# Weight slabs from one array in order of use, the low half written over the landed slab, four landing slots

## The reference

```
# first block, layers 0 and 1
mix = diff_moba_mixer(x, ...) if l == 0 else gla_mixer(x, ...)
x = layer_norm(DEEPNORM_ALPHA * x + mix, ln_mix_g[l], ln_mix_b[l])
x = layer_norm(DEEPNORM_ALPHA * x + sqrelu_mlp(x, ffn_w1[l], ffn_w2[l]), ...)
# diff_moba_mixer: x @ w_in (3072 columns), rope, 4 differential heads, 4 plain heads, @ w_out
# gla_mixer: x @ w_in (3088), gated linear attention, rms_norm, silu gate, @ w_out
# sqrelu_mlp: square(relu(x @ w1)) @ w2, 4096 hidden

# second block, layers 0 and 1
x = x + axial_gqa_attention(rmsnorm(x), w_qkv, ..., w_o)       # layer 0
x = x + multiscale_pool_mixer(rmsnorm(x), pool_w, pool_scale)  # layer 1
x = x + memory_cross_attention(rmsnorm(x), rmsnorm(mem), w_q, w_kv, w_o)
x = x + conv_gated_ffn(rmsnorm(x), w_up, conv_w, conv_b, w_down)   # 2 x 2816 up
```

## Time and profile before

| | us |
|---|---|
| median of 3 runs | 1413.38 (1412.26 to 1413.78) |
| profiled execution, first to last instruction | 1409.8 |
| PE busy | 1355.4 (96%) |
| DVE busy | 871.6 (62%) |
| ACT busy | 661.7 (47%) |
| POOL busy | 110.3 (8%) |
| mean granted TensorE clock | 0.992 |

### The profile page before, as it was taken

One profiled execution on the slowest core, in us unless ns is written; L12 is line 12 of the kernel. 1 busy time (PEld: TensorE's weight loads), 2 busy tenths in 40 slices (PEclk: granted clock), 3 DMA queues, 4 the chain that ended last, 5 costly groups with the idle time before them and its releaser, 6 DMA issues.

```text
span 1409.8 us, 20784 instructions
## 1 busy us (share of the span) xinstructions
PE 1355.4 (96%) x8456; PEld 1195.9 (85%) x8456; DVE 871.6 (62%) x936; ACT 661.7 (47%) x777; POOL 110.3 (8%) x146
## 2 busy tenths in 40 slices
PE   8978999999999999999997999999999999999997
PEld 5866899997987899999884788899999998899996
DVE  3767755556577755555577554776666544676664
ACT  3454444444743444444553352655555442555552
POOL 2031100000131100000113000100000100000000
PEclk9999999999999999999998999999999999999999
DMA  7650655555452565553741052565556452366551
GB/s 236 202 210 30 210 196 191 179 184 174 155 170 95 197 206 188 197 181 120 230 173 60 31 194 90 174 206 188 188 197 211 165 163 77 120 211 208 179 179 60
DMA packets 149326, 233.42 MB, mean 166 GB/s; under 512 B 3992, under 2 KB 103568, under 8 KB 149264
## 3 DMA queue, kind: packets, MB, share of 16 engines
q1 hardware_dynamic: 144640, 217.07, 46.6%
q0 software_dynamic: 4336, 14.77, 3.1%
q10 hardware_dynamic: 288, 0.72, 0.1%
HBM read 231.49 MB, written 1.05 MB: 165 GB/s over the span
## 4 chain that ended last, share of the span: by engine, by line
PE 81%; DVE 8%; DMA 4%; ACT 4%; issue 2%; POOL 1%; POOLq 0%; SPq 0%; DVEq 0%; ACTq 0%
PE ps L1598 13%; PE ps L1603 13%; PE ps L1599 13%; PE ps L1617 7%; PE ps L1618 7%; PE ps L1619 7%; PE ps L1550 3%; DMA raw<-in_hy_w_in 3%; PE ps L1552 3%; PE ps L1551 3%; DVE wl L956 2%; PE ps L1577 2%; PE ps L1579 2%; PE ps L1578 2%; PE ps L1777 2%; ACT wh L596 2%
## 5 line engine op out<-in xcount | busy, mean ns | idle before, releaser
L956 DVE TENSOR_TENSOR wl<-raw,wh 128x2048 fp32r<-128x2048 f32 x201 | 461.0, 2296 | 290.9 <-ACT wh L596 290.7
L596 ACT ACTIVATE wh<-raw 128x2048 fp32r<-128x2048 f32 x205 | 392.1, 1915 | 270.6 <-PE ps L1603 90.0
L1598 PE MATMUL ps<-xh,wh 128*128 128x256 f32 x1544 | 380.0, 284 | 3.0 <-DVE xl L969 2.3
L1599 PE MATMUL ps<-xh,wl 128*128 128x256 f32 x1544 | 378.7, 283 | 0.0
L1598 PEld LDWEIGHTS ps<-xh,wh 128*128 128x128 f32 x1544 | 295.9, 192 | 6.5 <-issue 4.3
L1599 PEld LDWEIGHTS ps<-xh,wl 128*128 128x128 f32 x1544 | 296.1, 192 | 2.1 <-issue 0.2
L1603 PE MATMUL ps<-xl,wh 128*128 128x256 f32 x1544 | 216.7, 283 | 0.0
L1603 PEld LDWEIGHTS ps<-xl,wh 128*128 128x128 f32 x1544 | 199.2, 192 | 0.0
L1617 PE MATMUL ps<-wh,hh 128*128 128x512 f32 x432 | 168.8, 391 | 0.4 <-DVE hl L1153 0.4
L1618 PE MATMUL ps<-wl,hh 128*128 128x512 f32 x432 | 168.7, 390 | 0.0
L1619 PE MATMUL ps<-wh,hl 128*128 128x512 f32 x432 | 168.1, 389 | 0.0
(11 more groups left out here) (212 smaller groups left out, 1499.3 us busy)
## 6 DMA issues: line engine op xcount, KB each, us to landing
raw<-in_ffn_w SPq DMA_DIRECT2D x64, 1024.0 KB, 5.2
raw<-in_ffn_w_up SPq DMA_DIRECT2D x44, 1024.0 KB, 5.1
raw<-in_ffn_w_down SPq DMA_DIRECT2D x22, 1024.0 KB, 5.0
raw<-in_xattn_w_kv SPq DMA_DIRECT2D x16, 1024.0 KB, 5.3
raw<-in_gla_w_in SPq DMA_DIRECT2D x13, 1024.0 KB, 5.3
raw<-in_hy_w_in SPq DMA_DIRECT2D x12, 1024.0 KB, 5.2
raw<-in_xattn_w_q SPq DMA_DIRECT2D x8, 1024.0 KB, 5.5
raw<-in_xattn_w_o SPq DMA_DIRECT2D x8, 1024.0 KB, 5.2
```

What stands on the lines that cost most here:

```text
L596: nc.scalar.activation(wh[:, s % RING, :], raw[:, s % RAWS, :], ACT.Copy).then_inc(wh_ready, 1)
L956: nc.vector.tensor_tensor(wl[:, s % RING, :], raw[:, s % RAWS, :], wh[:, s % RING, :].bitcast(F32), ALU.subtract)\
L1598: nc.tensor.matmul(o, wa[:, kt, cs], xh[:, kt, :], start=(kt == 0), stop=False)
L1599: nc.tensor.matmul(o, wb[:, kt, cs], xh[:, kt, :], start=False, stop=False)
```

## The change

The host lays the 205 slabs out in the order of use as one array `w_slabs` of 205 x 128 x 2048, so that every load is one block with 8 KB in a row for each partition; the function `slabs` builds it outside the measured time, and the thirteen weight arrays are no longer given to the device. `raw` has no memory of its own any more: it is the same memory as `wl`, seen as float32, with four slots (LOWS). The low half is written in place over the landed slab. So a load of slab s waits until TensorE has used slab s-4, not until slab s-2 is split. 16 KB on each partition are free. The addresses in SyncE's loops are gone with its loops, and since four slots must be counted in whole turns, the FFN loops take 6 groups a turn instead of 2 and the loop over the hybrid projection is written out.

```diff
-RAWS = 2
+LOWS = 4
 LOOKAHEAD = 3
+TURN = 12
...
-        raw = sb("raw", [P, RAWS, SLAB])
         wh = sb("wh", [P, RING, SLAB], F32R)
-        wl = sb("wl", [P, RING, SLAB], F32R)
+        wl = sb("wl", [P, LOWS, SLAB], F32R)
+        raw = nc.alloc_sbuf_tensor_at("raw", [P, LOWS, SLAB], F32, offset=nc.sbuf_base - 4 * LOWS * SLAB)
...
-            def load(s, src, view, i=None, step=0):
-                if s >= RAWS:
-                    sp.wait_ge(wl_ready, at(i, step, s - RAWS + 1))
-                sp.dma_start(view(raw, s % RAWS), src).then_inc(raw_loaded[s % RAWS], 16)
...
+            def load(s):
+                if s >= LOWS:
+                    sp.wait_ge(slab_used, s - LOWS + 1)
+                sp.dma_start(raw[:, s % LOWS, :], d["w_slabs"][s]).then_inc(raw_loaded[s % LOWS], 16)
...
+            for s in range(S):
+                load(s)
...
 # ScalarE, split
-                act.wait_ge(raw_loaded[s % RAWS], at(i, 16 * dstep // RAWS, 16 * (s // RAWS + 1)))
+                act.wait_ge(raw_loaded[s % LOWS], at(i, 16 * dstep // LOWS, 16 * (s // LOWS + 1)))
                 if s >= RING:
                     act.wait_ge(slab_used, at(i, dstep, s - RING + 1))
-                nc.scalar.activation(wh[:, s % RING, :], raw[:, s % RAWS, :], ACT.Copy).then_inc(wh_ready, 1)
+                nc.scalar.activation(wh[:, s % RING, :], raw[:, s % LOWS, :], ACT.Copy).then_inc(wh_ready, 1)
...
 # VectorE, split
-                nc.vector.tensor_tensor(wl[:, s % RING, :], raw[:, s % RAWS, :], wh[:, s % RING, :].bitcast(F32), ALU.subtract)\
+                nc.vector.tensor_tensor(wl[:, s % LOWS, :], raw[:, s % LOWS, :], wh[:, s % RING, :].bitcast(F32), ALU.subtract)\
...
 # the FFN loops of ScalarE, VectorE and TensorE
-                with act.Fori(0, (SQ_GROUPS - 2) // 2) as i:
-                    for g in (1, 2):
+                n = (SQ_GROUPS - 2) // (TURN // 2)
+                with act.Fori(0, n) as i:
+                    for g in range(1, 1 + TURN // 2):
...
+def slabs(a):
+    def cols(w, n0):
+        return [w[:, n0:n0 + T].reshape(KT, P, T)]
+    def chunk(w, n0):
+        return [w[k:k + 4 * P, n0:n0 + CH].reshape(4, P, CH) for k in (0, 4 * P)]
+    def rows(w, g):
+        return [w[g * T:(g + 1) * T].reshape(2, P, D)]
...
+    return np.stack([w.transpose(1, 0, 2).reshape(P, SLAB) for w in out])
```

More of the change, by code:

```diff
@@ L226, in bank4, with pair @@
             return ps[b][:, :].rearrange("p (a t) -> p a t", t=P)
[L228 to L235, removed]
+        def pair(s, n):
+            return [v.rearrange("p (k n) -> p k n", n=n) for v in (wh[:, s % RING, :], wl[:, s % LOWS, :])]
         def two(v, s):
             return v.rearrange("p h (n a s) -> p (h n) a s", a=2, s=s)
-        raw_loaded = [sem(f"raw_loaded{i}") for i in range(RAWS)]
+        raw_loaded = [sem(f"raw_loaded{i}") for i in range(LOWS)]
         wh_ready = sem("wh_ready")
@@ L697, in ffn @@
                 group(0)
-                with act.Fori(0, (SQ_GROUPS - 2) // 2) as i:
-                    for g in (1, 2):
-                        split(s0 + 2 * g - 1 + LOOKAHEAD, i, 4)
-                        split(s0 + 2 * g + LOOKAHEAD, i, 4)
+                n = (SQ_GROUPS - 2) // (TURN // 2)
+                with act.Fori(0, n) as i:
+                    for g in range(1, 1 + TURN // 2):
+                        split(s0 + 2 * g - 1 + LOOKAHEAD, i, TURN)
+                        split(s0 + 2 * g + LOOKAHEAD, i, TURN)
                         group(g, i)
+                for g in range(1 + n * TURN // 2, SQ_GROUPS - 1):
+                    splits(stage, 2 * g - 1, 2 * g + 1)
+                    group(g)
                 g = SQ_GROUPS - 1
@@ L756, in _ @@
             nat = ar(A_NAT, TT, 3072)
[L757 to L762, removed]
+            for c in range(6):
                 splits(g, 2 * c, min(2 * c + 2, 11))
@@ L1157, in ffn @@
                 group(0)
[L1158 to L1161, removed]
+                n = (SQ_GROUPS - 2) // (TURN // 2)
+                with dve.Fori(0, n) as i:
+                    for g in range(1, 1 + TURN // 2):
+                        split(s0 + 2 * g - 1 + LOOKAHEAD, i, TURN)
+                        split(s0 + 2 * g + LOOKAHEAD, i, TURN)
                         group(g, i)
+                for g in range(1 + n * TURN // 2, SQ_GROUPS - 1):
+                    splits(stage, 2 * g - 1, 2 * g + 1)
+                    group(g)
                 g = SQ_GROUPS - 1
@@ L1532, in stay_warm, with chunk_a @@
                     nc.tensor.matmul(ps[bank][:, :], zero_bf[:, 0:P], zero_bf[:, :], start=True, stop=True)
-            def chunk_a(stage, c, j, i=None, cstep=0, free=None, base=0, between=None):
+            def chunk_a(stage, c, j, free=None, base=0, between=None):
                 for half in range(2):
                     s = stage.s0 + j + half
-                    slab(s, i, 2 * cstep)
-                    wa, wb = slab_a(wh, s % RING), slab_a(wl, s % RING)
+                    slab(s)
+                    wa, wb = pair(s, CH)
                     for t in range(TT):
                         if half == 0:
-                            pe.wait_ge(bank_free, at(i, 2 * cstep, (stage.f0 if free is None else free) + 2 * c + t + 1))
+                            pe.wait_ge(bank_free, (stage.f0 if free is None else free) + 2 * c + t + 1)
                         if free is None and c == 0:
@@ L1588, in slab_up @@
                 slab(s, i, step)
-                wa, wb = slab_b(wh, s % RING), slab_b(wl, s % RING)
+                wa, wb = pair(s, T)
                 if stage:
@@ L1611, in down_part @@
             def down_part(s, par, t, c, last=False):
-                wa, wb = slab_dn(wh, s % RING), slab_dn(wl, s % RING)
+                wa, wb = pair(s, D)
                 o = ps[4 + 2 * c + t][:, :]
@@ L1805, in _ @@
             stay_warm(14, 4)
-            with pe.Fori(0, 3) as i:
-                for c in range(2):
-                    chunk_a(st["hy_in"], c, 2 * c, i, 2)
+            for c in range(6):
+                chunk_a(st["hy_in"], c, 2 * c)
             pe.wait_ge(cw_loaded, 16 * 8)
@@ L2026 @@
         arrays[f"ffn_norm{l}"] = a["ffn_norm_2"][l]
+    arrays["w_slabs"] = slabs(arrays)
+    for name in STREAMED:
+        del arrays[name]
     arrays.update(constants())
```

104 lines of the change are left out of this document (60 added, 44 removed).

## The result

The changed kernel takes 1473.74 us (median of 4 runs, 1468.09 to 1476.16) against 1413.58 us (1412.26 to 1413.95). The ratio is 1.042, 95% interval 1.040 to 1.044. That is 60 us slower; 1467 had been forecast, in a range of 1440 to 1487.

The account below looks back on a forecast made before the run. TensorE, busy 1355.4 of 1409.8 us, was taken to bound the kernel. Waits less the start's gain summed to +41.9, the clock +14: +56, 1469 from the 1413.4 median; 1467 was put forward, range 1440 to 1487.

Parts of the forecast that it names:

- The rule of the loads: Slab s is issued only once slab s-4 is used, so its split comes a whole landing later, 4.9 us alone.
- The two LayerNorms: Behind output projections, the LayerNorm part queued behind the second split starts 4.5 us later, twice: +9.0 us.
- The cross attentions: At the start of cross attention, twice, an exponential stands behind the late split: +4.05 and +4.3, together 8.35 us.
- Gated linear attention: Only the last level's step on VectorE has no level to spare and ends late: +2.85 us.
- The ends and small places: Ends of FFN and conv stages, passage from memory keys to second cross attention, query-key-value stage: together +8.4 us.
- The residuals: Residual sum and RMS norm behind an output projection, three times, wait for the late split: +4.85 each, +14.5 us.
- The FFN groups: In 30 groups the late split delays the hidden part just past TensorE's need: +0.09 each, +2.5 us in all.
- The start: Four slots empty at the start remove TensorE's waits for slabs 2 and 3 and a late split: -3.7 us.
- The clock: New idle stretches drop TensorE's granted clock to 0.50; six drops of 2.3 us: +14 us, ends 0 and 20.
- a short landing: Rival: 8 KB rows land in 4.4 us, so waits shrink and the FFN term goes: 1446 to 1456 us, chance 0.10.
- full clock: Rival: the waits come but TensorE's clock holds, +42: 1455 us, chance 0.17.
- the FFN stages fall behind: Rival: a landing takes 5.4 us, each of 30 FFN groups loses 0.4 and other terms grow: 1485 us, chance 0.12.

Follow-up runs that it names:

- the old rule: Changed kernel with two landing slots of its own again, slab s loaded when slab s-2 is split: 1409.07 us, ratio 0.998 to the kernel before.
- the kernel with the new order: Changed kernel, four slots in place, with the splits moved behind the urgent work on ScalarE and VectorE: 1428.11 us, ratio 1.0102 to the kernel before.

## Why the prediction was right

**The rule of the loads** was the cause, and the landing the one assumed, 4.9 us. Two one-sided edits show it: the rule alone makes the loss on the old layout, and the new layout without the rule does not. One sentence went too far: before, a slab was not always "long there" when its turn came, since 54 splits waited for loads, 138.7 us in all. At the places of the earlier trace rows the releaser is PE, and there it held.

**The two LayerNorms**: 9.0 forecast, 5.2 + 4.9 = 10.1 measured. **The cross attentions**: 8.35 and 8.5. **Gated linear attention**: 2.85 and 2.8; that the levels before the last have a level to spare held. **The ends and small places**: 8.4 and 9.7.

**The residuals**: 14.5 and 4.4 + 5.2 + 4.8 = 14.4. The residual sum comes as late as I had worked out, and TensorE with it.

**The FFN groups** were mis-sized: 2.5 and 6.6 us. I had taken the 0.12 us by which the hidden part is late, less what the next group takes up, as the cost of a group. Measured, the groups alternate, one at 11.3 us and the next at 11.4 to 12.0, and the mean, 11.48 and 11.41, is 0.19 to 0.26 above the 11.22 of before, twice or three times the 0.09 that I took. Part of the working stood on nothing: the 0.18 us "for the signal" is in no row, and where TensorE waited for VectorE it started 0.05 to 0.15 us after VectorE's end. The term was called steep, and at a landing of 5.2 us, on the old layout, it was about twice as large again.

**The start**: -3.7 and -4.75, for a reason that was in part wrong. The contiguous rows give most of it, and the start scatters by more than the difference of the two numbers.

**The clock**: 14 and 13 by the trace, but not from the six drops that I counted. Nine are new; those between the waits of the second and third residual cost nothing, and the others 1.3 to 2.6 us each. The trace of before had a row that I overlooked: a drop at 744.5, with waits of only 1.39 and 1.51 us around it, so the clock falls after waits far shorter than the 6.45 us of the earlier trace rows, too. The two waits, and the window of the drop (its PEclk is the 0.76, the mean of 1.00 and 0.50):

```profile
742.92 1.09 PE L1708 MATMUL ps<-con,arena 128*128 128x128 f32 x8 [1.39 <-DVE arena L1429]
745.52 2.04 PE L1725 MATMUL ps<-qk 128*128 128x512 f32 x2 [1.51 <-DVE qk L1083]
...
744.00:745.00 1.00, 0.01 (x1) 0.00 (x0) 0.97 (x3) 0.98 (x2) 1.00 (x1) 0.76 0.00 0
```

The sum was 56 and came out at 60; the number put forward, 1467, is 54 above the kernel before. The FFN groups alone are 4.1 us of the difference, and the other errors (+1.1, +0.15, +1.3, -1.05 and -1) nearly cancel, which is luck. Of **the rivals**, a short landing is refuted by the 4.9 us of the page, full clock by the mean of 0.976, and a start gain alone by the time. That the FFN stages fall behind was right in kind, with half its size and at a landing of 4.9 instead of 5.4. The fit in the Trainium skill (DMA: Bandwidth & Descriptors, Anatomy of one DMA), which the prediction puts at 4.4 us, is one for DMAs issued by GpSimd. These are issued by SyncE and landed in 4.9.

Of the signs, three did not come as written. ScalarE's waits for DMA are 2.9 us in the mean (477.4 us in 163 waits), not 4.9. TensorE has four new waits of over 4 us (5.92, 5.87, 4.35 and 5.46), not seven. And PEclk digits do not fall below 9 where the drops are: a slice of the page, 37 us, is too long to show one.

## What to carry to other kernels

A load that starts later costs nothing while every engine that it feeds has other work to do. It costs about its whole latency (here 4.4 to 5.2 us at the LayerNorms and residuals, at a landing of 4.9) wherever an engine that works in order waits for it with urgent work behind and nothing to spare, and part of it where there is some to spare (2.8 us in gated linear attention). Before giving up buffers, list what is written behind each wait: here moving those waits back returned 46 of 60 us, and two more slots, 16 KB on each partition, returned all of it. And look at what the loads are tied to: with loads tied to the preparation of a slab, moving the preparation moves the loads.

## What the runs showed of the hardware

- Contiguous rows of 8 KB instead of 1 to 4 KB cut the packets from 149326 to 34775, but the landing of 1 MB only from 5.0 to 5.5 us (medians of the groups on the page) to 4.9. The load queue's share of the DMA engines went from 46.6% to 44.2% with the old rule, where the span is the same to 0.3%; the 42.0% of the changed kernel are over a longer span.
- TensorE's clock fell to 0.50 after waits of 2.2 to 5.9 us (for instance at 151.71, and in the earlier trace rows for before), but in gated linear attention also behind waits of 1.67 and 1.07 us, which stand at the same places before without a drop; there a wait of 2.61 us had come 10 us earlier. Behind the first FFN it fell at 352 us in the kernel with the new order, after waits of 1.61 and 0.34 us, and did not in the changed kernel after 1.75 and 0.34. What made it fall there was not tried.
- VectorE reading and writing the same slot took 2294 ns, with source and target apart 2296 ns.
